# A two-layer mixture-of-experts decoder trunk: a weight piece in borrowed places, norm rows behind expert loads, and a reordered layer boundary

## The reference

```
mod = silu(c) @ ada_w[l] + ada_b[l]          # shift, scale, gate for attention and experts
h = x * (1 + scale_a) + shift_a              # modulated stream
y = attention(h) @ w_o
x = layer_norm(ALPHA * x + (1 + gate_a) * y) * ln_g + ln_b
h = x * (1 + scale_f) + shift_f
probs = softmax(h @ router_w)                # each token: 2 experts of one group of 4
m = sum over the 2 experts of gate * ((silu(h @ w_gate[e]) * (h @ w_up[e])) @ w_down[e])
x = layer_norm(ALPHA * x + (1 + gate_f) * m) * ln_g + ln_b
```

## Time and profile before

| | |
|---|---|
| median of 3 runs | 898.19 us (897.6 to 899.9) |
| the profiled execution | 900.95 us, span 899.3 us |
| busy: PE, DVE, ACT, POOL | 834.7, 376.0, 127.1, 90.3 us |
| mean granted TensorE clock | 0.986 of full |
| read from HBM | 302.49 MB, 338 GB/s over the span |
| weight queue of SP | 80.6% of the DMA engines' span |

### The profile page before, as it was taken

One profiled execution on the slowest core, in us unless ns is written; L12 is line 12 of the kernel. 1 busy time (PEld: TensorE's weight loads), 2 busy tenths in 40 slices (PEclk: granted clock), 3 DMA queues, 4 the chain that ended last, 5 costly groups with the idle time before them and its releaser, 6 DMA issues.

```text
span 899.3 us, 10792 instructions
## 1 busy us (share of the span) xinstructions
PE 834.7 (93%) x3730; PEld 393.0 (44%) x3730; DVE 376.0 (42%) x927; ACT 127.1 (14%) x341; POOL 90.3 (10%) x146
## 2 busy tenths in 40 slices
PE   6899999999998998899979999999999999889984
PEld 3584675435333333333328557654533333333331
DVE  2185867475211221222148688828521122212215
ACT  1001243011100000000010114611110000010010
POOL 1000000051110001011004000215111110000000
PEclk9999999999999999999999999999999999999998
DMA  8999982019999999999999799405499999999901
GB/s 352 431 421 426 399 329 95 1 59 431 426 428 426 425 427 426 427 426 426 425 384 419 299 426 425 175 0 213 163 406 424 428 424 427 426 427 426 392 12 47
DMA packets 23408, 304.59 MB, mean 339 GB/s; under 512 B 2720, under 2 KB 3232, under 8 KB 5280
## 3 DMA queue, kind: packets, MB, share of 16 engines
q1 hardware_dynamic: 22752, 303.14, 80.6%
q10 hardware_dynamic: 576, 0.40, 0.1%
HBM read 302.49 MB, written 1.05 MB: 338 GB/s over the span
## 4 chain that ended last, share of the span: by engine, by line
PE 68%; DMA 21%; DVE 8%; issue 2%; POOL 1%; ACT 1%; POOLq 0%; DVEq 0%; ACTq 0%
PE ps L1724 17%; DMA ring<-in_moe_w_up_dram 12%; PE ps L1732 7%; PE ps L1558 6%; PE ps L1529 6%; PE ps L1542 6%; PE ps L1642 5%; PE ps L1737 4%; DMA stream<-in_moe_w_up_dram 3%; DMA ring<-in_ada_w_dram 3%; DMA ring<-in_moe_w_down_dram 3%; PE ps L1453 1%; PE ps L1431 1%; PE ps L1705 1%; PE ps L1465 1%
## 5 line engine op out<-in xcount | busy, mean ns | idle before, releaser
L1724 PE MATMUL ps<-ring,hT 128*64 128x512 f32 x384 | 172.4, 599 | 11.8 <-DMA ring<-in_moe_w_up_dram 9.9
L1725 PE MATMUL ps<-ring,hT 128*64 128x512 f32 x384 | 172.7, 600 | 0.0
L1233 DVE TENSOR_TENSOR arena<-arena,ps 128x256 f32<-128x256 f32 x32 | 13.5, 421 | 233.8 <-ACT arena L802 126.8
L1724 PEld LDWEIGHTS ps<-ring,hT 128*64 128x64 f32 x384 | 51.1, 138 | 117.4 <-issue 117.4
L1732 PE MATMUL ps<-ring,arena 128*64 128x512 f32 x208 | 94.8, 599 | 0.0
L1733 PE MATMUL ps<-ring,arena 128*64 128x512 f32 x208 | 94.8, 598 | 0.0
L414 DVE SCALAR_TENSOR_TENSOR spare<-ring,csig,spare 128x512 f32<-128x512 f32 x112 | 86.1, 769 | 3.8
L1737 PE MATMUL ps<-arena 128*128 128x512 f32 x144 | 66.6, 605 | 3.2 <-DVE arena L1242 3.2
L1724 PE MATMUL ps<-spare,hT 128*64 128x512 f32 x128 | 58.9, 609 | 2.7 <-DMA stream<-in_moe_w_up_dram 2.5
L1725 PE MATMUL ps<-stream,hT 128*64 128x512 f32 x128 | 58.9, 610 | 0.0
L1529 PE MATMUL ps<-hT,ring 128*128 128x256 f32 x256 | 57.2, 386 | 1.5 <-ACT hT L680 1.5
(11 more groups left out here) (281 smaller groups left out, 1083.3 us busy)
## 6 DMA issues: line engine op xcount, KB each, us to landing
ring<-in_moe_w_down_dram SPq DMA_DIRECT2D x26, 2048.0 KB, 21.8
ring<-in_ada_w_dram SPq DMA_DIRECT2D x24, 2048.0 KB, 14.7
ring<-in_moe_w_gate_dram SPq DMA_DIRECT2D x24, 2048.0 KB, 18.4
ring<-in_moe_w_up_dram SPq DMA_DIRECT2D x24, 2048.0 KB, 21.3
spare<-in_moe_w_gate_dram SPq DMA_DIRECT2D x8, 2048.0 KB, 23.2
stream<-in_moe_w_up_dram SPq DMA_DIRECT2D x8, 2048.0 KB, 25.3
ring<-in_fox_w_in_dram SPq DMA_DIRECT2D x6, 2048.0 KB, 9.8
ring<-in_kv_ada_w_dram SPq DMA_DIRECT2D x4, 2048.0 KB, 13.8
```

The source lines that it names most:

```text
L1724: t.matmul(ps[0:CAP, bank, :], lhs(k), wcols(ng)[:, k, :], start=(k == 0), stop=(k == KC - 1))
L1725: mm = t.matmul(ps[CAP:P, bank, :], lhs(k), wcols(nu)[:, k, :], start=(k == 0), stop=(k == KC - 1))
```

## The change

- The second output piece of layer 0 gets a place of its own, number 8 (`HALVES`), made of four parts of 1024 elements: the two norm rows, block 1 of `h`, and `fold`. It is loaded by four transfers after the first readers of these are done. Expert piece 0 takes the place that it leaves, and the next ones shift by one.
- `norm_rows(0)` moves from ahead of the first output piece to behind the third expert piece, with a wait for the end of the second output piece.
- The gate product over that piece is four VectorE instructions of 1024 elements instead of two of 2048.
- `gained` waits for each block by itself, takes block 0 first, and stands ahead of `number_slots`. `residual(l, b)` waits for b + 1 counts of `x_ready`.
- `turned`: ScalarE copies all eight chunks of block 0 and four of block 1, VectorE four of block 1.
- `turn_stream(1)`: three idle matmuls, block 0, three eighths of `mod_product(4)`, block 1, then the other five. The product moves to bank 0, and `turn_mod(4, 0)` goes behind the first unit of keys.
- In an overflow round the transposes of `oput` stand ahead of the wait for ScalarE's copy, and the two gate products of 512 elements on half the partitions become one on all, from a copy of the gates (`gate_halves`) made once per layer.

The core of the diff:

```diff
-        s = free.pop(0)
+        s = HALVES if n == N_WO[0][1] else free.pop(0)
...
-    HT_N = (4, 12, 20, 28, 36)
+    HT_N = ((4, 4), (16, 8), (28, 12), (36, 20), (48, 24))
...
-            return {2: 6, 3: 0}.get(gi, 7)
+            return {2: 6, 3: 0, 4: 0}.get(gi, 7)
...
+        def quarter_pieces():
+            return [lnw[:, 0, :], lnw[:, 1, :], h[:, 1, :], fold[:, :, :].rearrange("p a n -> p (a n)")]
...
+            def load_quarters(n):
+                for s_ in range(2):
+                    sp.wait_ge(ht_ready[s_], HT_N[0][s_])
+                sp.wait_ge(f_steps, 1)
+                for q, part_ in enumerate(quarter_pieces()):
+                    sp.dma_start(part_, pieces[n][:, 1024 * q:1024 * q + 1024]).then_inc(full[HALVES], 16)
...
+                        if l == 0 and 6 * i + j == 3:
+                            spent(sp, N_WO[0][1])
+                            norm_rows(0)
                         if TURN[n]:
                             sp.wait_ge(used[SLOT[n]], TURN[n])
...
-                if n == N_WO[0][0]:
-                    norm_rows(0)
...
                 pool.wait_ge(lw_in, 32 * (norm + 1))
-                pool.wait_ge(xn_r, 4 * (norm + 1))
-                for b in (1, 0):
+                for b in range(NB):
+                    pool.wait_ge(xn_r, 4 * norm + 2 * b + 2)
...
-            number_slots(0)
             gained(0)
+            number_slots(0)
...
-            number_slots(1)
             gained(2)
+            number_slots(1)
...
                 if norm == 1:
-                    mod_product(4, range(0, 5))
+                    idle_work(3, 7)
...
                     if b and norm == 1:
-                        mod_product(4, range(5, KC))
+                        mod_product(4, range(0, 3))
...
+                if norm == 1:
+                    mod_product(4, range(3, KC))
...
-                pe.wait_ge(x_ready, 2 * NB * l + 2 - b)
+                pe.wait_ge(x_ready, 2 * NB * l + b + 1)
...
-                            for q, rows in enumerate((slice(0, 64), slice(64, P))):
-                                d.tensor_tensor(oy[rows, :], ps[rows, 7, :], gbc[rows, 1, 512 * q:512 * q + 512],
-                                                ALU.mult).then_inc(o_dve, 1)
+                            d.tensor_tensor(oy, ps[:, 7, :], gate_halves, ALU.mult).then_inc(o_dve, 1)
```

More of the change, by code:

```diff
@@ L105, in build @@
     SPARES = 2
+    HALVES = RING + SPARES
     SLOT, TURN = [], []
-    turns, free = [0] * (RING + SPARES), list(range(RING))
+    turns, free = [0] * (RING + SPARES + 1), list(range(RING))
     for n in range(len(pieces)):
@@ L117, in build @@
         turns[s] += 1
-        free.append(s)
+        if s != HALVES:
+            free.append(s)
     COLS_C, COLS_ADA, COLS_LN, COLS_NORMG, COLS_BF = 0, KC, KC + 7 * 2 * KC, KC + 7 * 2 * KC + 8 * KC, KC + 7 * 2 * KC + 8 * KC + 1
@@ L238, in build @@
         oy = part(P, 512)
+        gate_halves = part(P, 512)
         oputT = fold[:, 1, 0:S]
@@ L251, in build @@
         ogu = mrow[:, 1, :]
-        full = [sem(f"full{i}") for i in range(RING + SPARES)]
-        used = [sem(f"used{i}") for i in range(RING + SPARES)]
+        full = [sem(f"full{i}") for i in range(RING + SPARES + 1)]
+        used = [sem(f"used{i}") for i in range(RING + SPARES + 1)]
         res_mm = sem("res_mm")
@@ L356, in landed @@
         def landed(eng, n):
-            eng.wait_ge(full[SLOT[n]], 16 * (TURN[n] + 1))
+            eng.wait_ge(full[SLOT[n]], (64 if SLOT[n] == HALVES else 16) * (TURN[n] + 1))
         def spent(eng, n):
@@ L390, in wcols, with out_rows @@
             return room(n).rearrange("p (k n) -> p k n", k=KC)
+        def quarter_pieces():
+            return [lnw[:, 0, :], lnw[:, 1, :], h[:, 1, :], fold[:, :, :].rearrange("p a n -> p (a n)")]
+        def out_rows(n, q):
+            if SLOT[n] == HALVES:
+                return [a_.rearrange("p (k n) -> p k n", k=2) for a_ in quarter_pieces()[2 * q:2 * q + 2]]
+            return [wcols(n)[:, k:k + 2, :] for k in (4 * q, 4 * q + 2)]
         def wdown(n):
@@ L647, in _ @@
             inv_std(0)
+            gained(0)
             number_slots(0)
-            gained(0)
             windows(0)
@@ L658, in _ @@
             inv_std(2)
+            gained(2)
             number_slots(1)
-            gained(2)
             windows(1)
@@ L704, in turned @@
                 for b in range(NB):
[L705 to L708, removed]
+                    for k in range(KC if b == 0 else 4):
+                        if k % 4 == 0:
+                            act.wait_ge(ht_mm, 4 * norm + 2 * b + k // 4 + 1)
                         modulated(hT[:, k, b * P:(b + 1) * P], turned_bank(b, k), m, k).then_inc(ht_ready[0], 1)
@@ L955, in turned @@
             def turned(m):
[L957 to L961, removed]
+                dve.wait_ge(ht_mm, 4 * M_NORM[m] + 4)
+                for k in range(4, KC):
+                    modulated(hT[:, k, P:2 * P], turned_bank(1, k), m, k).then_inc(ht_ready[1], 1)
             def turned_again(m):
@@ L1030, in gate_weights @@
                 landed(dve, n)
-                w = wcols(n)[:, 4 * q:4 * q + 4, :]
-                d.tensor_tensor(w, w, gbc[:, 0, 512 * s_:512 * s_ + 512].unsqueeze(1).broadcast_to([P, 4, 512]),
-                                ALU.mult).then_inc(wo_r, 1)
+                g_ = gbc[:, 0, 512 * s_:512 * s_ + 512].unsqueeze(1)
+                if SLOT[n] != HALVES:
+                    w = wcols(n)[:, 4 * q:4 * q + 4, :]
+                    d.tensor_tensor(w, w, g_.broadcast_to([P, 4, 512]), ALU.mult).then_inc(wo_r, 1)
+                    return
+                for at, w in enumerate(out_rows(n, q)):
+                    ins = d.tensor_tensor(w, w, g_.broadcast_to([P, 2, 512]), ALU.mult)
+                    if at:
+                        ins.then_inc(wo_r, 1)
+                    else:
+                        link(ins)
             def diff_norm(hd):
@@ L1278, in experts @@
                 overflow_tables(l)
+                for q, rows in enumerate((slice(0, 64), slice(64, P))):
+                    link(d.tensor_copy(gate_halves[rows, :], gbc[rows, 1, 512 * q:512 * q + 512]))
                 for i in range(PAIRS):
@@ L1502, in turn_stream @@
                         pe.wait_ge(xn_r, 4 * norm + 2 * b + s_ + 1)
-                        if norm == 1 and b and s_:
-                            pe.wait_ge(mod_row, 4)
                         for k in range(4 * s_, 4 * s_ + 4):
@@ L1526, in turned_units @@
                     for cc in range(4):
+                        if u == UNITS0 + 1:
+                            turn_mod(4, 0)
                         unit_free(u)
@@ L1769, in overflow @@
                             gate_up_strips(i, j).then_inc(o_pe, 1)
+                            pe.wait_ge(o_dve, k + 3)
+                            for bb in range(NB):
+                                mm = t.transpose(ps[:, 7, bb * P:(bb + 1) * P], oput[:, bb, :], ident[:, :])
+                            mm.then_inc(o_pe, 1)
                             pe.wait_ge(o_act, g * 2 + 1)
-                            pe.wait_ge(o_dve, k + 3)
                             for q in range(4):
@@ L1775, in overflow @@
                             mm.then_inc(o_pe, 1)
-                            for bb in range(NB):
-                                mm = t.transpose(ps[:, 7, bb * P:(bb + 1) * P], oput[:, bb, :], ident[:, :])
-                            mm.then_inc(o_pe, 1)
                             pe.wait_ge(o_dve, k + 6)
@@ L1903, in _ @@
             stream_turned(2)
-            turn_mod(4, 0)
             u = turned_units(UNITS0, N_K[1], hT)
```

25 lines of the change are left out of this document (15 added, 10 removed).

## The result

| | before | after |
|---|---|---|
| median, runs side by side | 899.05 us (897.6 to 903.79, 4 runs) | 910.56 us (908.64 to 913.79, 4 runs) |
| ratio, 95% interval | | 1.0119 [1.0084, 1.0154] |
| profiled execution, span | 900.95 us, 899.3 us | 908.64 us, 907.0 us |
| granted TensorE clock | 0.986 | 0.977 |

What follows compares the result with a forecast made beforehand. TensorE sets the pace, except in layer 0's experts, where transfers at the 426 GB/s ceiling do. Terms 0.4 + 11.0 - 5.1 + 0 - 1.8 = +4.5 us on 898.19 give 902.7 us, range 896 to 907.

Steps and rivals of the forecast that it cites:

- wait for x, layer 0: Layer 0, before the experts: late norm rows hold up x, so residual, counts, tables, gather and experts move 22.0 us.
- low clock behind it: Layer 0, after TensorE's pause: residual, counts and first zeroed matmuls run at the low clock, 2.4 us (bounds 0 and 4).
- last piece of group 4 lands: End of layer 0's experts: the last transfer of modulation group 4 moves by 11.0 us, to 471.3.
- keys: Layer boundary: key matmuls start 5.9 us later, 11.0 of late transfer less 5.1 gained at the boundary.
- x by block, layer 1: Layer 1's route: GpSimd starts earlier but holds up VectorE's norms; put at 0, bounds -1.3 and +0.6 us.
- last wait and overflow rounds: Layer 1's two overflow rounds on TensorE's path: 0.9 us saved each, -1.8 us (bounds -1.4 and -3.4).
- The stage end: End of layer 0's experts: TensorE done at 466 to 469, the transfer still last by a little, at 471.3.
- 5.1 us of gain: Layer boundary: landing to keys shrinks from 13.9 to 8.8 us, block 0 transposed during the wait (bounds 3.5 and 5.5).
- early piece: Layer 0's queue: expert piece 0 issued near 142 takes 4.9 us from the full stretch, but the pause swallows it.
- Rival 3: Layer 0's queue: norm rows get through beside the weights; 894.4 us, or 889 with no pause; 12%, with other faster causes.
- rival 4: Layer 0: piece 0 is not early because the output piece's place binds; time as forecast, no chance given.
- Rival 2: Layer boundary: VectorE's group 5 sums meet GpSimd's x, bind keys 2 us, clock low again; 904.5 to 908 us, 13%.

Runs made afterwards that it cites:

- e8: The changed kernel with 24 more zeroed matmuls in layer 0's route, in TensorE's long pause: 906.87 us, 1.0066 of the kernel before.
- e2: The changed kernel with GpSimd waiting for all four halves of the norm before forming x: 906.6 us, 1.0069 of the kernel before.
- e6: The kernel before with the overflow round's edits alone: 898.18 us, 0.9973 of the kernel before.
- e1: The changed kernel with the norm rows loaded ahead of the first up piece: 893.37 us, 0.9920 of the kernel before.
- e4: The changed kernel with four instead of eight zeroed matmuls behind the logits in layer 1's route: 907.66 us, 1.0083 of the kernel before.
- e11: The changed kernel with the norm rows behind one waiting weight piece instead of two: 903.94 us, 1.0049 of the kernel before.
- e9: The kernel before with the layer boundary's and the overflow round's edits alone: 894.5 us, 0.9937 of the kernel before.
- e3: The changed kernel with norm rows ahead of the first up piece and GpSimd awaiting both norms: 890.24 us, 0.9889 of the kernel before.
- e10: The changed kernel with norm rows ahead of the first up piece and x whole in layer 1 only: 889.96 us, 0.9873 of the kernel before.
- e14: The changed kernel with the old order of forming x and norm rows ahead of the first up piece: 890.1 us, 0.9893 of the kernel before.

## Why the prediction was wrong

| step | foretold | measured |
|---|---|---|
| gate product, borrowed place | +0.4 | TensorE reaches its wait at 201.00, before 200.95 |
| wait for x, layer 0 | 22.0 | 21.1 (residual 222.05) |
| low clock behind it | 2.4 | 2.0 (e8) |
| first expert matmul | +24.4 | +23.15 |
| next piece of the queue lands | 256.6 | 255.7 |
| last piece of group 4 lands | 471.3 | 471.0 |
| keys | +5.9 | +7.8, and 0.6 for `turn_mod` |
| x by block, layer 1 | 0 (-1.3 to +0.6) | +4.85 in the profile, +4.0 by e2 |
| last wait and overflow rounds | -1.8 (-1.4 to -3.4) | -5.6 in the profile, -2.5 by e6 in all |
| sum | +4.5 | +7.7 in the profiles |
| kernel before, to which the sum is added | 898.19 | 900.7 to 901.1 in 90 executions |

The forecast of 902.7 us lies 7.9 under the measured 910.56: 3.2 us by the terms of the sum, 2.5 because the median of three executions of the kernel before was a low one, and 2.2 that no term accounts for.

**The step that failed** is "x by block in layer 1", put at 0 and measured at 4.0 to 4.85 us. The prediction had the mechanism: both norms held by one of GpSimd's instructions each, so that route starts 3.4 us later. The row of DVE shows just that, 2.5 us for each, and in e1, where the clock did not fall, the scores start 3.5 us later than before, counted from the first transposes behind attention. The prediction then set 2.9 us against it, since route's later instructions would run free, and so counted VectorE's time as if all of it lay on the path. It does not. Counted in the same way, the first expert matmul of e1 is still 3.1 us late (34.4 us, before 31.2), so 0.3 us came back. Under x whole, the 3.4 us of held instructions lie beside TensorE's sixteen idle matmuls of 7.1 us. By block, the norm delays the scores, the idle matmuls start behind them, and the chain goes over TensorE (e4). In the changed kernel TensorE's clock also fell behind the two waits, 1.7 us more; the prediction had no term for that here. The Trainium skill ("SBUF — State Buffer", section Who interferes with whom) gives the lock on the shared ports, and the trace agrees with it, 4.98 us against 1.00; the fault was in what stands behind each instruction held.

**The wait for x in layer 0 was right**, to a microsecond, and e11 confirms its working. The prediction said too that `residual(0, 1)` waits for both blocks, but it did not price that edit by itself. It is 4.7 us of the 21. With layer 1's share, putting back the old order of x takes away the loss (901.55 us for 910.56); moving the norm rows forward takes away more (893.37).

**The stage end was taken from the wrong engine.** The experts ended at 470.3, not between 466 and 469. Two waits for transfers, of 0.93 and 2.08 us, stayed, and the overflow round met a lower clock. The transfer itself came when foretold, at 471.0. But TensorE then still had the norm and the transposes of block 0 ahead of the product, 3.5 us from the end of the experts, where the prediction had them hidden behind the transfer: the keys came 1.9 us later than foretold. The 5.1 us of gain also counted the moved `turn_mod` as saved, though it is only paid later, 0.6 us. The 8.8 us from the product's start to the keys were nearly right (8.2 here and in e9).

**Luck helped.** The overflow's edit is worth 2.5 us in the medians, inside its bounds; the profiles' 5.6 hold the low clock that before happened to have there. Without that the terms would have missed by some 3 us more. The early piece was "worth nothing" only because of the pause, as foretold; in time it is worth 4.3.

**The rivals.** Rival 3's price for rows in time was 889 us; e3, e10 and e14 measured 890, by moving the rows instead of by a faster queue. That is near by luck: the gain is 10.5 us from 900.7 (4.3 for the place, 3.7 for the boundary, 2.5 for the overflow's edits), and not 8.9 from 898.19. The changed kernel itself is none of the rivals; rival 4 is ruled out by the gate piece at 141.67. Rival 2 had GpSimd and VectorE colliding in the wrong place, at the boundary instead of in layer 1's route.

**What stays open**: the 2 to 4 us between the difference of the profiles and that of the medians. It goes with the granted clock of the executions (0.977 to 0.968 as the span goes from 907.0 to 912.1 us), but why the changed kernel's clock varies so was not tried.

The best versions, e10, e14 and e3, are at 890 us, 1.1 to 1.3% faster than before. They keep every other part of the change; only the place of the norm rows and the order or the waits of x differ.

## What to carry to other kernels

A load that is moved down a queue waits for everything that the loads ahead of it wait for. So for a small transfer with an engine behind it, write down the waits of each issue that it is moved past; here one line made 17 us. When an instruction is held by another engine, its price is not the time held but what stands behind it: 4 us on a norm cost 3 to 4, and 3.4 us on two table instructions left a wait of 0.2, since the engine behind them was filling time meanwhile. And filler matmuls put in to keep the clock become the bound as soon as what they wait for is late.

## What the runs showed of the hardware

- Norm rows of 512 KB behind two weight pieces of 2.1 MB landed at 212.5, behind one at 207.6: 4.9 us a piece, no passing (in the changed kernel the second piece at 209.8, the gain row at 211.0, the bias row at 212.5).
- A VectorE norm of two instructions of 128x512 in SBUF took 4.97 us while GpSimd formed x beside it, and 1.00 alone: each lasted about as long as one of GpSimd's multiplies or adds (2.34 us).
- After a pause of 21 us of TensorE the granted clock was 0.50 for 4 us (four matmuls in 3.78 us instead of 1.88). With idle matmuls in the pause they took 1.99.
- The clock is not the same from one kernel to the next after equal pauses. Behind waits of 1.90 and 1.83 us the next four idle matmuls took 3.58 us in the changed kernel, with a granted clock of 0.66 in the stretch around them, and 1.88 in e1 behind waits of the same lengths:

```profile
629.00:634.00 5.00, 4.88 (x24) 1.93 (x24) 1.43 (x5) 0.00 (x0) 4.78 (x3) 0.66 0.02 3
```

```profile
606.57 0.66 PE L1535 MATMUL ps<-ident,stream 128*128 128x128 f32 x4 [1.90 <-DVE stream L1102]
609.06 0.66 PE L1535 MATMUL ps<-ident,stream 128*128 128x128 f32 x4 [1.83 <-DVE stream L1102]
609.55 1.88 PE L1734 MATMUL ps<-arena,ones 128*128 128x512 f32 x4
```
